# A diffusion trunk step: earlier squares, decay tables behind the first projections, and GpSimd on two output chunks

## The reference

```python
def _rmsnorm(x, g):
    y = x32 * lax.rsqrt(jnp.mean(x32 * x32, axis=-1, keepdims=True) + EPS)
    return y * g
for l in range(DEPTH):
    mc = _modulation(c, w_mod[l], b_mod[l])           # six vectors: silu(c) @ w_mod + b_mod
    h = _rmsnorm(x, norm_mix[l]) * (1.0 + mc[1]) + mc[0]
    z = h @ w_in[l]                                    # q, k, v of A and B (attention), C (retention), gates
    # A: differential attention, with rotated q, k; B: neighbourhood or full attention;
    # C: retention in both directions, with decays exp(log_sigmoid(ret_decay) * distance)
    x = x + mc[2] * (sum_i sigmoid(gate_i) * (o_i @ w_proj_i)) @ w_out[l]
    h = _rmsnorm(x, norm_ffn[l]) * (1.0 + mc[4]) + mc[3]
    x = x + mc[5] * expert_choice_ffn(h)               # each of 16 experts takes its top tokens
y = _rmsnorm(x, norm_final)
```

## Time and profile before

| | us |
|---|---|
| median of 3 runs | 2028.72 (2028.66 to 2030.94) |
| the profiled execution | 2027.77 |
| its span, first to last instruction | 2025.7 |
| TensorE busy | 1867.7 (92%) |
| VectorE, ScalarE, GpSimd busy | 592.7, 341.0, 60.4 |
| mean DMA rate over the span | 273 GB/s of 552.38 MB |
| mean granted clock of TensorE | 0.995 |

### The profile page before, as it was taken

One profiled execution on the slowest core, in us unless ns is written; L12 is line 12 of the kernel. 1 busy time (PEld: TensorE's weight loads), 2 busy tenths in 40 slices (PEclk: granted clock), 3 DMA queues, 4 the chain that ended last, 5 costly groups with the idle time before them and its releaser, 6 DMA issues.

```text
span 2025.7 us, 19626 instructions
## 1 busy us (share of the span) xinstructions
PE 1867.7 (92%) x8214; PEld 938.6 (46%) x8214; DVE 592.7 (29%) x1160; ACT 341.0 (17%) x787; POOL 60.4 (3%) x47
## 2 busy tenths in 40 slices
PE   5999999999999988888789999999999998888886
PEld 2565556555544333233345655565555343333323
DVE  1232447545221111101132324654533102010102
ACT  4022331100211101000141322210003010100102
POOL 1100000000000000000030000000000000000000
PEclk9999999999999999999999999999999999999998
DMA  9322272442589999999972221716225999999995
GB/s 389 152 94 88 84 307 78 166 166 77 208 365 428 429 429 429 430 429 428 426 309 94 83 88 57 287 42 249 110 102 245 396 429 428 429 429 428 429 429 243
DMA packets 53544, 552.38 MB, mean 273 GB/s; under 512 B 5840, under 2 KB 10832, under 8 KB 12240
## 3 DMA queue, kind: packets, MB, share of 16 engines
q1 hardware_dynamic: 49680, 548.51, 65.2%
q10 hardware_dynamic: 3776, 2.62, 0.4%
HBM read 546.91 MB, written 4.19 MB: 272 GB/s over the span
## 4 chain that ended last, share of the span: by engine, by line
PE 65%; DMA 29%; DVE 3%; ACT 2%; issue 1%; POOL 0%; SPq 0%; POOLq 0%; DVEq 0%; ACTq 0%
PE psum L943 12%; DMA ring<-in_w_up 12%; PE psum L1115 12%; DMA ring<-in_w_down 12%; PE psum L802 11%; PE psum L1027 6%; PE psum L804 6%; PE psum L1040 4%; DMA wide<-in_w_gate 3%; PE psum L397 2%; DMA ring<-in_w_gate 2%; PE psum L862 1%; PE psum L765 1%; PE psum L1095 1%; PE psum L1163 1%
## 5 line engine op out<-in xcount | busy, mean ns | idle before, releaser
L943 PE MATMUL psum<-hT,ring 128*128 128x384 f32 x768 | 255.8, 486 | 0.0
L802 PE MATMUL psum<-hT,ring 128*128 128x384 f32 x720 | 244.4, 493 | 7.2 <-ACT dense L1295 5.1
L1115 PE MATMUL psum<-dense 128*64 128x512 f32 x864 | 195.4, 596 | 30.8 <-DMA dense<-in_w_up 17.6
L1115 PE MATMUL psum<-ring,dense 128*64 128x512 f32 x832 | 188.2, 596 | 26.9 <-DMA ring<-in_w_gate 16.0
L943 PEld LDWEIGHTS psum<-hT,ring 128*128 128x128 f32 x768 | 145.7, 190 | 100.9
L802 PEld LDWEIGHTS psum<-hT,ring 128*128 128x128 f32 x720 | 135.8, 193 | 96.5 <-issue 6.6
L1115 PEld LDWEIGHTS psum<-dense 128*64 128x64 f32 x864 | 62.5, 137 | 153.6 <-issue 129.1
L1027 PE MATMUL psum<-dense,ring 128*128 128x384 f32 x384 | 131.9, 487 | 0.0
L1805 DVE TENSOR_TENSOR state<-state,psum 128x512 f32<-128x512 f32 x32 | 22.0, 688 | 373.2 <-PE psum L1115 335.2
L804 PE MATMUL psum<-ring,hT 128*128 128x512 f32 x288 | 126.5, 592 | 0.0
L1115 PEld LDWEIGHTS psum<-ring,dense 128*64 128x64 f32 x832 | 59.8, 137 | 140.7 <-issue 119.1
(11 more groups left out here) (211 smaller groups left out, 1680.2 us busy)
## 6 DMA issues: line engine op xcount, KB each, us to landing
ring<-in_w_up SPq DMA_DIRECT2D x32, 2048.0 KB, 38.2
ring<-in_w_in SPq DMA_DIRECT2D x60, 1024.0 KB, 8.6
dense<-in_w_up SPq DMA_DIRECT2D x30, 2048.0 KB, 40.0
ring<-in_w_down SPq DMA_DIRECT2D x30, 2048.0 KB, 40.1
dense<-in_w_gate SPq DMA_DIRECT2D x24, 2048.0 KB, 35.6
wide<-in_w_down SPq DMA_DIRECT2D x20, 2048.0 KB, 40.2
ring<-in_w_gate SPq DMA_DIRECT2D x20, 2048.0 KB, 36.7
wide<-in_w_gate SPq DMA_DIRECT2D x20, 2048.0 KB, 38.1
```

Source lines behind the costliest of these rows:

```text
L802: last = M.matmul(psum[:, bank, 0:T], ring[:, n % RING, k, cols], hT[:, k, :], start=k == 0, stop=k == KD - 1)
L943: last = M.matmul(psum[:, Z[1], 0:T], ring[:, n_gate % RING, k, (j % 4) * P:(j % 4 + 1) * P], hT[:, k, :], start=k == 0, stop=k == KD - 1)
L1115: last = M.matmul(psum[HALF * half:HALF * (half + 1), bank, :], lhsT(k), w[:, kk, half * SLAB:(half + 1) * SLAB], start=k == 0, stop=k == ...
```

## The change

Five things are changed.

1. **Squares.** There are three buffers for squares in place of two. GpSimd adds four squares; TensorE takes the squares 4, 5 and 6 first, then the sum, then square 7.
2. **Layer starts.** In layer 0 four column groups are begun with the first chunks, the first of them ahead of a transpose; in layer 1 two groups are begun, slab 1's product stands ahead of the norm's sum, and slab 3's product right behind it. In the ring the first projection slab changes places with modulation slab 3.
3. **Decay tables.** VectorE's part stands behind the second rotation; ScalarE's three parts behind the reads of the groups 4, 5 and 6.
4. **The norm ahead of the router.** TensorE's first modulation product stands behind the sum, and ScalarE's read of it behind the inverse root.
5. **The output.** GpSimd multiplies the chunks 6 and 7 by the weight, in place, once they are squared, and by the inverse root when it is there. VectorE does six chunks.

```diff
-ADDED = 6
+ADDED = 4
+BEGUN = (4, 2)
+POOL_SCALES = (6, 7)
...
+        squared = [square[:, 0, :], square[:, 1, :], tmp[:, 1, :]]
...
         START_FILL = [[("mod", 0, 0), ("modT", 0, 0), ("mod", 0, 2), ("modT", 0, 2), ("mod", 0, 1), ("modT", 0, 1), ("mod", 0, 3), ("modT", 0, 3)],
-                      [("mod", 1, 1), ("modT", 1, 1), ("mod", 1, 3), ("modT", 1, 3)]]
+                      [("mod", 1, 1), ("mod", 1, 3), ("modT", 1, 1), ("modT", 1, 3)]]
...
+        FIRST_SLABS = [[("mod", 0), ("mod", 2), ("mod", 1), ("w_in", 0), ("mod", 3)], [("mod", 1), ("mod", 3), ("w_in", 0)]]
...
                 load_slab(0, 2)
+                load_half(0, 3, 0)
                 wait_slab_free(sp, 0, 0)
-                load_half(0, RING, 0)
-                load_slab(0, 3)
-                load_half(0, RING, 1)
+                load_slab(0, RING)
+                load_half(0, 3, 1)
...
+                for k in POOL_SCALES:
+                    pool.wait_ge(sq_ready, 2 * KD * DEPTH + k + 1)
+                    G.tensor_scalar(xT[:, k, :], xT[:, k, :], final_gain[:, k:k + 1], None, ALU.mult).then_inc(y_gained, 1)
+                pool.wait_ge(rs_ready, 2 * DEPTH + 1)
+                for k in POOL_SCALES:
+                    pool.wait_ge(y_gained, POOL_SCALES.index(k) + 1)
+                    G.tensor_tensor(xT[:, k, :], xT[:, k, :], rs[:], ALU.mult).then_inc(y_pool, 1)
...
-                    pe.wait_ge(sq_added, count(sq_added, (mixer + 1) * ADDED))
-                    M.matmul(psum[:, bank, 0:T], ones, sum_sq, start=True, stop=False)
                     for k in range(ADDED, KD):
+                        if k == KD - 1:
+                            pe.wait_ge(sq_added, count(sq_added, (mixer + 1) * ADDED))
+                            M.matmul(psum[:, bank, 0:T], ones, sum_sq, start=False, stop=False)
                         pe.wait_ge(sq_ready, count(sq_ready, mixer * KD + k + 1))
-                        last = M.matmul(psum[:, bank, 0:T], ones, square[:, k % 2, :], start=False, stop=k == KD - 1)
+                        last = M.matmul(psum[:, bank, 0:T], ones, squared[k % 3], start=k == ADDED, stop=k == KD - 1)
...
-                    fill(CHAIN_FILL[layer][0:1])
                     norm_sum(TR[0], 1)
-                    fill(CHAIN_FILL[layer][1:3])
+                    fill(CHAIN_FILL[layer][0:3])
...
-                        if 2 <= k < ADDED + 2:
-                            sc.wait_ge(sq_added, at(sq_added, mixer * ADDED + k - 1))
-                        elif k >= 2:
-                            sc.wait_ge(sq_summed, at(sq_summed, mixer * (KD - ADDED) + k - ADDED - 1))
+                        if 3 <= k < ADDED + 3:
+                            sc.wait_ge(sq_added, at(sq_added, mixer * ADDED + max(2, k - 2)))
+                        elif k >= 3:
+                            sc.wait_ge(sq_summed, at(sq_summed, mixer * (KD - ADDED) + k - ADDED - 2))
...
                     for g in range(Z_FIRST):
                         read_z(layer, g)
+                        if g == 4:
+                            decay_logs()
+                        if g == 5:
+                            decay_inside()
+                        if g == 6:
+                            decay_across()
...
                     squares(layer, 1)
+                    inverse_rms(TR[0], 2)
                     read(CHAIN_FILL[layer][0:1])
-                    inverse_rms(TR[0], 2)
                     modulate(1, scale_ffn, 24)
...
                     for c in range(8):
+                        if c == 2:
+                            decays()
...
-                for k in range(KD):
+                for k in range(KD - len(POOL_SCALES)):
                     V.scalar_tensor_tensor(out=xT[:, k, :], in0=xT[:, k, :], scalar=final_gain[:, k:k + 1], in1=rs[:],
```

More of the change, by code:

```diff
@@ L1318, in _ @@
                     else:
+                        read(START_FILL[layer][0:1])
                         inverse_rms(TR[0], 1)
@@ L1330, in _ @@
-                    A_.activation(decay_t[:, 2], decay_t[:, 1], ACT.Ln, bias=c_("one")).then_inc(ln_ready, 1)
-                    sc.wait_ge(decay_ready, at(decay_ready, 1))
-                    for h in range(HEADS_C):
-                        A_.activation(in_decay[:, h], c_("below"), ACT.Exp, scale=decay[:, h:h + 1])
-                        last = A_.activation(bwd_decay[:, h], c_("above"), ACT.Exp, scale=decay[:, 4 + h:5 + h])
-                    last.then_inc(decay_exp, 1)
-                    for d, (row, col) in enumerate((("since", "k_until"), ("until", "k_since"))):
-                        for c in range(2):
-                            for i in range(2):
-                                part = slice(64 * i, 64 * i + 64)
-                                h = 4 * d + 2 * c + i
-                                A_.activation(q_decay[part, d, c, :], c_(row)[part], ACT.Exp, scale=decay[part, h:h + 1])
-                        A_.activation(k_decay[:, d, :], decay[:, 4 * d:4 * d + 4], ACT.Exp, scale=c_(col))
@@ L1343, in _, with decay_logs @@
-                    for i in range(2):
-                        part = slice(64 * i, 64 * i + 64)
-                        last = A_.activation(chunk_decay[part], decay[part].rearrange("p (d c i) -> p d c i", d=2, c=2)[:, :, :, i],
-                                             ACT.Exp, scale=float(P))
-                    last.then_inc(chunk_ready, 1)
+                    def decay_logs():
+                        sc.wait_ge(lam_sum, at(lam_sum, 1))
+                        A_.activation(lamb[:, 2:4], lamb[:, 0:2], ACT.Exp).then_inc(lam_exp, 1)
+                        sc.wait_ge(abs_ready, at(abs_ready, 1))
+                        link(A_.activation(decay_t[:, 1], decay_t[:, 0], ACT.Exp, scale=-1.0))
+                        A_.activation(decay_t[:, 2], decay_t[:, 1], ACT.Ln, bias=c_("one")).then_inc(ln_ready, 1)
```

98 lines of the change are left out of this document (60 added, 38 removed).

## The result

| | before | after |
|---|---|---|
| median | 2029.6 us (4 runs, 2028.66 to 2030.94) | 2009.76 us (4 runs, 2008.83 to 2010.12) |
| profiled execution, its span | 2027.77, 2025.7 | 2010.12, 2008.3 |
| mean granted clock | 0.995 | 0.998 |

The ratio is 0.9901, with a 95% interval of 0.9884 to 0.9918. The forecast was 2011.8 us, in a range of 2007.5 to 2018.5. The forecast is 2.0 us above the median, and two of its five terms are off by more than half a microsecond, in opposite directions.

What follows compares the result with a forecast made beforehand. Bound by TensorE and expert-slab loads tied to TensorE's progress. Terms 6.1 + 7.7 + 0.2 + 3.6 - 0.7 = 16.9 us took 2027.77 to 2010.9; 0.95 for the median gave 2011.8 us, range 2007.5 to 2018.5.

Steps and rivals of the forecast that it cites:

- Layer 0's start: First modulation work to fifth projection group in layer 0: 6.1 us won, bounds 3 and 7.1.
- Layer 1's start: Layer 1's norm to fifth group: 7.7 us won (norm 1.3, moved product 1.9, tables' stall 3.4, rest slow clock).
- my own pool: TensorE's idle time plus slow-clock cost over the layer starts: 8.5 us in layer 0, 10.8 in layer 1.
- Norms ahead of the router: Sum ends 0.8 us earlier, but ScalarE's slab read limits it: 0.1 us won a layer, bounds -0.2 and 0.8.
- The last norm: Norm behind the last expert: fewer GpSimd additions, 3.6 us won, or 0.6 if all ten passes run at 1.2 GHz.
- The output: Final multiplies split between VectorE and GpSimd: 0.7 us lost; bounds 0.7 won with no conflict, 1.0 lost fully in turn.
- The clock: Rival: norms of layer 1 and of the end run at 1.2 GHz throughout, costing 3.2 + 3.0, so 2018.0 us; chance 0.12.
- The tables land elsewhere: Rival: held rotations or ScalarE's pieces reach TensorE, 3 us a layer, so 2017.8 us; chance 0.08.
- two-group slack: Layer starts: TensorE needs a rotation's result two groups (11 us) on, so a held rotation of 10.5 us just fits.
- More is won: Rival: router's norm keeps its 0.8 us twice and engines don't meet at the output, so 2009.0 us; chance 0.12.
- The product that blocks TensorE's queue: Rival: slab product ahead of layer 1's norm waits for a late landing; 2031.8 us at 20 us late; chance 0.03.
- The stream of loads absorbs nothing: Answers the rival that expert loads absorb what is won ahead of them, so no change, 2028.7 us; chance 0.02.

Runs made afterwards that it cites:

- tables alone: The kernel before with only the move of the decay tables (VectorE's and ScalarE's parts): 2021.03 us, ratio 0.9964.
- the run without the second multiply: The kernel after, with GpSimd leaving out its multiplies of chunks 6 and 7 by the inverse root: 2009.02 us, one run.
- two edits: The decay tables' move alone on the kernel before, 2021.03 us; the kernel after with the tables back in their old place, 2023.76 us.

## Why the prediction was right, and where it was not

**Layer 0's start: 6.1 forecast, 6.09 measured.** The place is right, and the steps are: 53.1 was forecast for the fifth group with before's start, and it is 52.09 with a first slab that landed 1.05 earlier. But the agreement to the hundredth is luck, since this stage scatters by 1.5 us with the moment at which the clock rises, and at equal clock the gain would be nearer 6.6. One sentence of the reasoning was misleading: I took the 6.4 us that ScalarE spends on the tables for TensorE's stall. TensorE waited only 1.73 us there before. The tables become a stall of 6.57 us (5.5 without the late landing) when the new order brings TensorE to that point sooner, and this is why tables alone win 1.5 us. The forecast survived because I counted the new order forward, instruction by instruction, and did not add up gains of single edits.

**Layer 1's start: 7.7 forecast, 8.37 measured.** The sum ends 5.3 us behind the scatter (forecast 5.2), the first half starts 8.3 behind it (8.2). The difference comes after: eight transposes in a row take 0.88 us on the path, not 1.3, and the first half group 3.05, not 3.2. The step that put 1.9 us to the credit of the product moved into the wait for GpSimd is wrong, though: with four squares there is no such wait any more, and the product only delays the sum (with six, behind the product, 1.79 of the 3.62 us are left). Moving it behind wins 1.5 us. The credits were mis-set on the other side too: the 7.7 left 1.1 us for the slow clock, where my own pool had 3.6 and all of it came back (the window's clock is 1.00). The total hid both, since after-times were counted forward.

**Norms ahead of the router: 0.1 each forecast, 0.22 measured.** The place and the limit are right: ScalarE's modulation begins at 543.08, behind the slab's read. The small number is the difference of two larger ones, -1.5 for the order and +1.3 for the split.

**The last norm: 3.6 forecast, 3.32 measured.** GpSimd is no longer on the path and all passes run at full clock:

```profile
1995.46 0.81 PE L740 MATMUL psum<-tmp,const 128*128 128x384 f32 x2
1996.41 0.91 PE L740 MATMUL psum<-square,const 128*128 128x384 f32 x2
1997.16 0.81 PE L738 MATMUL psum<-tmp,const 128*128 128x384 f32 x2
1997.80 0.81 PE L740 MATMUL psum<-square,const 128*128 128x384 f32 x2
```

**The output: 0.7 lost forecast, 1.77 measured (1.40 without the landing), and this is outside my bounds of 1.0 lost to 0.7 won.** This is the mis-sized term. Both bounds failed at the queue of stores. The upper one names it, but lets it win 0.7 us with no conflict; it wins nothing, since two issues stand behind the sixth multiply (the run without the second multiply). The lower one prices the multiplies alone: the stores of chunks 6 and 7 stand last in SyncE's order, so two issues are added behind the slower multiplies. The conflict itself is real and somewhat smaller than priced: 4.74 us against 3.26 alone, and 5.3 fully in turn. In the timeline the two engines take turns, one instruction each (windows of one instruction; two of VectorE's, then GpSimd's two):

```profile
2000.35 1.35 DVE L1887 SCALAR_TENSOR_TENSOR xT<-xT,final_gain,rs 128x384 f32<-128x384 f32 x1
2001.62 1.34 DVE L1887 SCALAR_TENSOR_TENSOR xT<-xT,final_gain,rs 128x384 f32<-128x384 f32 x1
1999.86 1.42 POOL L726 TENSOR_TENSOR xT<-xT,rs 128x384 f32<-128x384 f32 x1 [0.93 <-ACT rs L1538]
2001.25 1.30 POOL L726 TENSOR_TENSOR xT<-xT,rs 128x384 f32<-128x384 f32 x1
```

VectorE's second and third multiply end 0.4 us behind the end of a GpSimd multiply. Its other four, one ahead and three once GpSimd is through, take 0.60 to 0.62. GpSimd's two take 1.42 and 1.30 us, against 1.0 for such an instruction alone. By the Trainium skill, SBUF — State Buffer, Who interferes with whom, a VectorE instruction with two SBUF inputs contends with a GpSimd instruction that reads SBUF, and the lock on the ports that they share is exclusive. The trace agrees for this pair, with a small overlap: the two GpSimd multiplies cost VectorE 1.48 us, and 2.0 was the price fully in turn. The direction is the rule's: the offload made the tail longer.

**The sum.** 16.9 us forecast, 17.4 between the spans: +1.05 from a first slab that landed earlier, +0.67 in layer 1, +0.24 at the routers, -0.28 at the last norm, -1.07 at the output. The first of these is no term of the forecast but scatter, and it hides the output's error; that the spans agree to 0.5 us is luck to this extent. The rest of the 2.0 us between forecast and median is in the executions: I put the median 0.95 us above the profiled one, and it is 0.36 below it, and 1.8 us stand around the span in place of 2.1.

**The rivals.** The clock: 1.00 in both norms, excluded. The tables land elsewhere: GpSimd's additions did hold VectorE, but TensorE never waited for a rotation there. GpSimd's two additions and VectorE's held instructions:

```profile
69.58 9.40 POOL L709 TENSOR_TENSOR wide<-wide,const 128x2048 f32<-128x2048 f32 x2
```

```profile
69.99 4.62 DVE L1632 TENSOR_TENSOR dense<-dense,tmp 128x256 f32<-128x256 f32 x1
...
75.12 4.15 DVE L1631 TENSOR_TENSOR dense<-dense,const 128x256 f32<-128x256 f32 x1
```

Two instructions of 0.43 us took 4.62 and 4.15, inside the two-group slack that the forecast relied on. More is won: no; its engines did meet at the output, and the router gave 0.22. The product that blocks TensorE's queue: the slab had landed, so no wait for it, but the 1.85 us that it occupies are on the path, which is the small form of that rival. The stream of loads absorbs nothing: 460.4 us from router to scatter in both kernels.

## What to carry to other kernels

Count a reordered stage forward from its first instruction, and don't add the gains of single edits: here two edits were worth 1.5 and -2.5 us alone (1.1 of the loss was a late landing) and 6.1 together. A split between two engines is a choice for each place, since it pays where the helper's last result is waited for (4.2 us at the last norm, half of it clock) and costs where the other engine's queue is the limit (0.9 us at each router). Ahead of handing the last multiplies to a second engine, look at what stands behind them: with eight stores of 0.4 to 0.5 us on one queue there was nothing to win, and 1.4 to 1.8 us to lose.

## What the runs showed of the hardware

- Stores of 192 KB that are ready when their turn comes start 0.37 to 0.50 us behind the one ahead of them on SyncE's queue, and are recorded with 0.43 to 0.46 us each; the others follow VectorE's multiplies, 0.53 us apart, and are recorded with 0.33 to 0.35. Moving two of the eight to ScalarE's queue shortened the tail by about 0.6 us (one profile each).
- The landing of the first weight slab scatters by 1.5 us between kernels (13.26 to 14.78 us from the span's start), and in the table above this moves all that follows.
- The granted clock rose 2.8 to 6.0 us behind TensorE's first product, in thirteen profiles. In the seven with the instructions of the kernel after, the lengths of layer 0's start, 37.41 to 38.94 us, stand in the same order.
- A VectorE and a GpSimd multiply of 128 x 384 floats with two SBUF inputs each took turns: 1.35 us in place of 0.61 on VectorE, 1.42 and 1.30 in place of 1.0 on GpSimd.
- The kernel before scatters over 10 us between executions (2024.84 to 2035.44 in 17 runs), at mean clocks from 0.996 down to 0.990, and the two longest have the lowest clocks; the kernel after scatters over 1.3 us at 0.997 to 0.999. So idle stretches, clock falls and scatter went together; that the one causes the other was not tested by itself.
